# Prompt attention of a hybrid decoder trunk: bias add and row maximum in one vector operation per bank, from a bias tile that POOL makes per head

## What is computed

```python
dist = (q_pos[:, None] - k_pos[None, :]).astype(jnp.float32)
slopes = alibi_slopes(DA_HEADS)
bias = jnp.where(dist >= 0, -slopes[:, None, None] * dist, -jnp.inf)
s1 = jnp.einsum('bqhd,bkhd->bhqk', q1, k1).astype(jnp.float32) * scale + bias
s2 = jnp.einsum('bqhd,bkhd->bhqk', q2, k2).astype(jnp.float32) * scale + bias
attn = jax.nn.softmax(s1, axis=-1) - lam * jax.nn.softmax(s2, axis=-1)
return jnp.einsum('bhqk,bkhv->bqhv', attn, v.astype(jnp.float32))
```

## Time and profile before

| | |
|---|---|
| median of three runs | 2865.07 us (2863.9 to 2873.49) |
| the profiled execution | 2858.58 us |
| its span on the core | 2856.8 us |
| PE busy | 2757.1 us, 97% of the span |
| DVE busy | 1390.2 us, 49% |
| ACT busy | 1026.7 us, 36% |
| POOL busy | 226.1 us, 8% |

### The profile page before, as it was taken

The page is one execution under the profiler, slowest core; times in us unless marked ns, Lnnn a source line. Parts: engine busy times, 40 slices in busy tenths (PEclk is TensorE's granted clock), DMA queues, the critical chain, the costliest instruction groups (busy, mean ns, idle before and its releaser), DMA issues.

```text
span 2856.8 us, 56783 instructions
## 1 busy us (share of the span) xinstructions
PE 2757.1 (97%) x23882; PEld 2602.8 (91%) x23882; DVE 1390.2 (49%) x1624; ACT 1026.7 (36%) x1155; POOL 226.1 (8%) x140
## 2 busy tenths in 40 slices
PE   7999999999899999999999999999998999999996
PEld 7999999976499999999999999989655999999996
DVE  5333346744666543333653333547356665333345
ACT  5343223312464343332343332333125633343222
POOL 0111001321000011100001100012300000111000
PEclk9999999997999999999999999999889999999998
DMA  4222232256622222222322222323656222222221
GB/s 150 93 88 80 91 124 91 75 173 191 204 96 89 89 89 94 92 81 85 104 89 97 94 72 92 131 76 115 183 174 192 89 82 96 88 88 79 91 96 59
DMA packets 119393, 304.61 MB, mean 107 GB/s; under 512 B 14930, under 2 KB 24914, under 8 KB 118738
## 3 DMA queue, kind: packets, MB, share of 16 engines
q1 hardware_dynamic: 119250, 302.57, 32.8%
HBM read 291.08 MB, written 11.44 MB: 106 GB/s over the span
## 4 chain that ended last, share of the span: by engine, by line
PE 84%; DVE 7%; DVEq 4%; ACT 3%; issue 1%; POOL 0%; DMA 0%; SPq 0%; ACTq 0%; POOLq 0%
PE ps L598 63%; PE ps L646 9%; PE ps L810 2%; DVE wlo L1550 2%; ACT whi L1169 1%; DVEq L1665 1%; PE ps L893 1%; DVEq L2021 1%; PE ps L865 1%; PE ps L959 1%; DVE mx L1879 1%; PE ps L697 1%; PE ps L878 1%; ACT L1169 1%; DVEq L1878 1%
## 5 line engine op out<-in xcount | busy, mean ns | idle before, releaser
L598 PE MATMUL ps<-Hh,whi 128*128 128x260 f32 x3456 | 694.8, 282 | 15.6 <-DVE Hl L1616 13.9
L598 PE MATMUL ps<-Hl,whi 128*128 128x260 f32 x3456 | 693.2, 282 | 0.0
L598 PE MATMUL ps<-Hh,wlo 128*128 128x260 f32 x3456 | 692.1, 282 | 0.0
L1169 ACT ACTIVATE whi<-raw 128x2048 fp32r<-128x2048 f32 (+2 forms) x225 | 395.8, 1759 | 723.2 <-PE ps L598 662.1
L1550 DVE TENSOR_TENSOR wlo<-raw,whi 128x2048 fp32r<-128x2048 f32 (+2 forms) x213 | 444.5, 2087 | 368.5 <-ACT whi L1169 368.4
L598 PEld LDWEIGHTS ps<-Hh,whi 128*128 128x128 f32 x3456 | 530.3, 188 | 16.8 <-issue 13.8
L598 PEld LDWEIGHTS ps<-Hl,whi 128*128 128x128 f32 x3456 | 532.5, 189 | 0.0
L598 PEld LDWEIGHTS ps<-Hh,wlo 128*128 128x128 f32 x3456 | 531.7, 188 | 0.0
L1169 ACT ACT_TABLE_LOAD x169 | 216.8, 1283 | 310.3 <-PE ps L598 231.5
L1550 DVE TENSOR_TENSOR ta<-ps,R 128x520 f32<-128x520 f32 x88 | 61.6, 700 | 475.9 <-PE ps L598 474.8
L598 PE MATMUL ps<-Gh,whi 128*128 128x260 f32 x1408 | 284.0, 283 | 0.0
(11 more groups left out here) (271 smaller groups left out, 3019.7 us busy)
## 6 DMA issues: line engine op xcount, KB each, us to landing
raw<-in_ffn_up SPq DMA_DIRECT2D x176, 512.0 KB, 4.2
raw<-in_ffn_down SPq DMA_DIRECT2D x128, 352.0 KB, 3.3
kb<-in_cache_k SPq DMA_DIRECT2D x128, 256.0 KB, 3.1
kb<-in_cache_v SPq DMA_DIRECT2D x128, 256.0 KB, 3.0
raw<-in_w_in SPq DMA_DIRECT2D x56, 512.0 KB, 4.4
raw<-in_w_gate SPq DMA_DIRECT2D x32, 512.0 KB, 4.8
raw<-in_w_ab SPq DMA_DIRECT2D x16, 512.0 KB, 4.4
raw<-in_w_o SPq DMA_DIRECT2D x16, 512.0 KB, 4.4
```

Of the source, the lines that this page charges most:

```text
L598: last = nc.tensor.matmul(ps[:, bank + 2 * m + c, 0:HT], w, x[:, k0 + k, c * HT:(c + 1) * HT], start=starts and k == 0 and n == 0, stop=st ...
L1169: return nc.scalar.activation(out, in_, func, **kw)
```

## The change

POOL makes one tile per head and layer, `bias` = distances x slope (128 x 512), in two buffers used in turn. The first lies where `Ke` was, which is dead once `kc1` is counted, the second where `NTl` was and `Osb` will be. POOL makes heads 0 and 1 after `kc1`, head 2 after `max03` and head 3 after `max13`, that is, when the last reader of the same buffer is done. On DVE, the two `scalar_tensor_tensor` and the `reduce_max` of an item give way to two `tensor_tensor_reduce`, each of which adds bias and scores, writes `sc`, and gives the maximum over its n columns as an accumulator output; one of the two drains goes. Each head's first item waits for its bias tile. Nothing else of the loop's order is changed.

```diff
--- before.py
+++ after.py
@@ -258,6 +258,7 @@
         Zx, Eb = (at(n, [P, SEQ], F32, tb_at + 2048 * m) for m, n in enumerate(("Zx", "Eb")))
         Es = at("Es", [P, PAST], F32, tmp_at)
         Osb = at("Osb", [P, SEQ], F32, scr_at + 13312)
+        bias = [at(f"bias{n}", [P, SEQ], F32, o) for n, o in enumerate((h_at + 2 * T * 4, scr_at + 13312))]
         qz = at("qz", [P, NSEQ * 129], F32, tb_at)
         vtok = at("vtok", [P, 2, SEQ], F32, tb_at)
         bkm = at("bkm", [16, 4, P], F32, pt_at)
@@ -380,6 +381,7 @@
         a_pe = track("a_pe", "vt0" + "".join(stage(i, "at", "vt", "score", "out") for i in range(NI + 2)) + " out3")
         a_dve = track("a_dve", " ".join((f"attn{item(i - 1)} " if i else "") + (f"max{item(i)}" if i < NI else "") for i in range(NI + 1)))
         a_act = track("a_act", "vt0" + "".join(stage(i, "at", "vt", "exp", "out") for i in range(NI + 2)) + " out3")
+        a_pool = track("a_pool", " ".join(f"b{h}" for h in range(H)))
         n_act = track("n_act", " ".join(f"rt{k - 1} sq{k} yh{k - 1}" if k else "sq0" for k in range(8)) + " rt7 yh7")
         n_pe = track("n_pe", " ".join(f"sum{k}" for k in range(8)))
         n_dve = track("n_dve", " ".join(f"y{k} yl{k}" for k in range(8)))
@@ -1539,6 +1541,14 @@
                 pool.wait_ge(d_pe.sem, d_pe.at("w51", L))
                 nc.gpsimd.memset(Pz[:, :, :], 0.0).then_inc(q_pool.on("pz", L), 1)
 
+                for h in range(H):
+                    if h > 1:
+                        pool.wait_ge(a_dve.sem, a_dve.at(f"max{h - 2}3", L))
+                    elif h == 0:
+                        pool.wait_ge(d_dve.sem, d_dve.at("kc1", L))
+                    nc.gpsimd.tensor_scalar(bias[h % 2][:, :], CM[:, M_DIST:M_DIST + SEQ], CC[:, C_SLOPE + h:C_SLOPE + h + 1], None, ALU.mult
+                                            ).then_inc(a_pool.on(f"b{h}", L), 1)
+
                 ffn(L, B_UP2, 1)
 
 
@@ -1871,12 +1881,11 @@
                         dve.wait_ge(a_pe.sem, a_pe.at(f"at{h}{q - 2}", L))
                     elif h:
                         dve.wait_ge(a_pe.sem, a_pe.at(f"at{h - 1}{q + 2}", L))
+                    if q == 0:
+                        dve.wait_ge(a_pool.sem, a_pool.at(f"b{h}", L))
                     for m in range(2):
-                        V.scalar_tensor_tensor(out=sc[:, q % 2, m, 0:n], in0=CM[:, M_DIST + SEQ - n:M_DIST + SEQ],
-                                               scalar=CC[:, C_SLOPE + h:C_SLOPE + h + 1],
-                                               in1=ps[:, 4 + m, 0:n], op0=ALU.mult, op1=ALU.add)
-                    dve.drain()
-                    V.reduce_max(mx[:, q % 2, :], sc[:, q % 2, :, 0:n], AXX)
+                        V.tensor_tensor_reduce(out=sc[:, q % 2, m, 0:n], in0=bias[h % 2][:, SEQ - n:SEQ], in1=ps[:, 4 + m, 0:n],
+                                               scale=1.0, scalar=NEG, op0=ALU.add, op1=ALU.max, accum_out=mx[:, q % 2, m:m + 1])
                     dve.drain()
                     V.tensor_scalar(nm[:, q % 2, :], mx[:, q % 2, :], -SCALE, None, ALU.mult).then_inc(a_dve.on(f"max{h}{q}", L), 1)
 
```

## The result

| | before | after |
|---|---|---|
| median of seven runs | 2865.95 us (2860.16 to 2876.82) | 2847.91 us (2842.5 to 2856.08) |
| ratio after / before | | 0.9929, 95% interval 0.9908 to 0.9951 |
| the profiled execution | 2858.58 us | 2846.88 us |

The change is faster by 0.7%, 20 us by the ratio; 13.1 us (0.46%) had been forecast. The same two kernels were compared once more at the end of the study, on another chip: 2850.28 us (ten runs) against 2862.28 (fourteen), ratio 0.9958, 0.9944 to 0.9972, that is 12 us. The two intervals overlap between 0.9944 and 0.9951. So the gain is certain, and its size is 12 to 20 us depending on which comparison one takes. The traces show where executions of one kernel differ, and they say more about the forecast's steps than the total does.

What follows compares the result with a forecast made beforehand. The kernel is bound by PE, the attention loop by a chain through PE, DVE and ACT. Per layer 1.05 + 3.52 + 1.97 = 6.5 us, 13.1 for two: 2865.07 - 13.1 = 2852 us, range 2847 to 2864.

Steps and rivals of the forecast that it cites:

- rival 1: On DVE, TTR needs two cycles per element because of its accumulator; 2864 us, or 2870 with a costly read; chance 0.12.
- Rival 2: In the loop, PE, ACT or `S` becomes late at the 512 item too; 6.5 us lost, 2858.5 us; chance 0.10.
- Rival 3: POOL's four tiles per layer each block DVE for 1.27 us, 10 us in all; 2862 us; chance 0.04.
- I take it as long as L1875: On DVE, each TTR takes as long as the L1875 it replaces: 0.74 us with 512 keys, 0.61 with 384.
- two reads are 0.18: On DVE, each item's two accumulator reads put off what follows by 0.09 us each, as on ACT.
- if the read is hidden: Upper bound of DVE's saving per item: reduce + 0.08, that is 0.50, 1.03 or 1.30 us; 16.2 in all.
- The gain should arrive undiminished: Everything behind the attention loop hangs on its end in the same order, so all 13.1 us reach the total.
- SP's loads … come earlier as these do: SP's loads wait for PE's steps and move earlier with them; no DMA is added or moved.
- Head 3's 1.97 us: Gain per layer from head 3's items on the path: 0.85 us with 384 keys plus 1.12 with 512.
- One with a single input should take no longer: A POOL bias tile takes at most the 1.27 us of a two-input operation; DVE's first item waits 0.1 us.
- the 0.2 that the prediction had named as a sign against it: DVE idle time put down to POOL's L1549 above 0.2 us would show the forecast wrong.
- rival 4: Shorter gaps keep PE's clock up in both layers' loops; time falls by more than 20 us further; chance 0.02.

Runs made afterwards that it cites:

- experiment 7: Kernel of experiment 5 with PE's state matmuls ahead of the transposes in all odd items; one execution, 2847.19 us.
- experiment 2: Changed kernel with the fused operation in the 512-key items alone, separate add and reduce in the others; 2852.12 us, ratio 0.9964 to the kernel before.
- experiment 3: Changed kernel with SP loading the last four groups of value pages from fixed numbers, without reading the page table; one execution, 2840.25 us.
- experiment 6: Kernel before the change, with page numbers read into SP's registers ahead of the buffer wait; 2860.82 us, ratio 0.9995.
- experiment 8: Kernel of experiment 7 with POOL's first tile made in two pieces, 128 columns first; 2847.74 us, ratio 0.9945 to the kernel before.
- experiment 9: Changed kernel with ACT issuing one group of pages and page numbers read ahead of SP's wait; 2845.52 us, ratio 0.9939 to the kernel before.
- experiment 5: Changed kernel with a group's four page numbers read into SP's registers ahead of the buffer wait; 2847.34 us, ratio 0.9944 to the kernel before.
- experiment 10: Kernel of experiment 9 plus POOL's first tile in two pieces and state matmuls ahead of transposes in items 3, 7, 11, 15; 2841.14 us, repeat 2839.92.

## Why the forecast was nearly right in the sum and wrong in three terms

**Right.** The loop is a chain, and the gain comes from the items of it, not from DVE's share: PE's busy time stayed, DVE's fell. The 384 item of heads 1 and 2 is held at 0.31 us by PE's L989, which is 0.32 as forecast, and that it is L989 is shown by experiment 7, where moving that matmul freed 0.37. The fused operation runs at full rate. With that rival 1 falls. Rival 2, PE, ACT or `S` late at the 512 item too, falls for heads 1 and 2 by experiment 2, where 1.40 + 0.24 should arrive and 1.65 did. In head 3 its outcome came by a wait that it didn't name, that for the last pages. Rival 3 falls: the later tiles are never waited for. With one source in PSUM the accumulator's form takes 1.03 ns a column. The Trainium skill's rule of half rate with two SBUF sources that aren't bf16 ("Vector Engine (DVE) Microarchitecture Reference", points that are easy to get wrong) doesn't hold in this trace for the plain form: L1891 has both sources in SBUF in fp32 and takes 0.75 us, full rate. TTR says nothing against it, since one source is in PSUM; no run here had the accumulator with both in SBUF.

**The price of TTR with its read: mis-sized.** The step was "I take it as long as L1875" and "two reads are 0.18". TTR is 0.06 shorter than L1875, twice per item, and the reads cost 0 instead of 0.18. Together 0.30 us per item on the path: 0.60, 1.12 and 1.40 us instead of 0.32, 0.85 and 1.12. The head distance, forecast at -1.76, was -2.39; over two distances in each layer that is 2.5 us of gain that the forecast lacked. The row for it stood in the trace of before, in the earlier trace rows: `S<-Sd,ps`, a plain sum of an SBUF and a PSUM stream of 512 columns on the same engine, takes 0.68 us against L1875's 0.74. It was read as the scan's business, and L1875 taken because it was the operation being replaced. For the read, ACT's row was taken as nearest "since it is the same kind of instruction"; on DVE it starts together with the next operation. The bound "if the read is hidden" was the right end; added up over the items on the path it gives 16.0 us for two layers, not the 16.2 of the prediction.

**"The gain should arrive undiminished" and "SP's loads … come earlier as these do": wrong.** Head 3's 1.97 us, with true prices 2.5, was lost in full. SP's loads do come earlier, as PE's release does, but the release is not moved by head 3's later items: it lies ahead of them, and the eight issues and the transfer behind it last 12.3 us in both kernels. The step looked for what waits for DVE, ACT and PE, and never followed the queue that fills `kb`. Experiments 3 and 6 show both sides: with shorter issues the 2.5 us arrive, and in the kernel before the same relief is worth nothing.

**POOL's tile: mis-sized.** "One with a single input should take no longer" than 1.27 us; it took 1.56. The wait was 0.54 instead of 0.1, above the 0.2 that the prediction had named as a sign against it, but only at a layer's first item. Experiment 8 removed it.

**The clock, given little.** From head 0 to head 1 the change saved 1.8 to 2.0 us. In layer 0 half of it is DVE's: from the first score operation of the 384 item to the end of its `sc` it is 4.58 us (696.98 to 701.56) instead of 5.58 (694.94 to 700.52). The rest comes behind that, where the chain is PE alone up to head 1's 384 item: 19.75 us instead of 20.71 for the same matmuls. Some of the transposes among them, at 1.2 GHz before, ran at the higher clock (chain rows, first before, then after):

```profile
700.57 0.90 PE ps L692 x3
...
711.90 1.05 PE ps L692 x4
```

```profile
701.61 0.55 PE ps L694 x3
...
712.55 0.59 PE ps L694 x4
```

Granted clock in windows of this stretch (columns of the earlier trace rows), first before, then after:

```profile
695.00:700.00 5.00, 3.74 (x14) 1.54 (x13) 4.61 (x12) 1.57 (x5) 0.00 (x0) 0.50 0.35 104
700.00:705.00 5.00, 4.43 (x25) 2.67 (x25) 3.69 (x7) 1.59 (x5) 0.00 (x0) 0.50 0.01 3
705.00:710.00 5.00, 5.00 (x27) 2.88 (x27) 2.63 (x8) 1.64 (x6) 0.00 (x0) 0.50 0.00 0
```

```profile
695.00:700.00 5.00, 4.65 (x24) 2.42 (x22) 3.76 (x13) 1.57 (x5) 0.00 (x0) 0.62 0.99 298
700.00:705.00 5.00, 3.39 (x21) 1.91 (x22) 3.13 (x11) 1.89 (x5) 1.56 (x1) 0.72 0.04 11
705.00:710.00 5.00, 5.00 (x28) 3.04 (x27) 2.14 (x10) 1.28 (x4) 0.00 (x0) 0.50 0.00 0
```

Before, PE runs at 0.50 (1.2 GHz) for about 24 us, from 689.5 to 713. After, the clock is up in between for some 4 us around 700, and about 17 us are left at 1.2 GHz. The rise in between, with PE idle for half of it, isn't what counts: in layer 0 of the repeat it is missing (0.50 from 692.3 to 712.8), and the stretch took 24.37 us as well. There too the low clock ended earlier in the work, 14.9 us behind the start of the 384 item, against 18.1 before. Nothing like the 20 us of rival 4 came of it, but the clock is a large source of spread: with the same DVE work the stretch took 22.9 us in both layers of experiment 3 and in layer 1 of experiment 9, 24.4 in the change, and 27.4 and 20.5 in the two layers of experiment 8. A difference of a few us between two profiled executions can come from here alone.

It doesn't explain why the two comparisons differ by 8 us. In all four traced loops of the change this stretch took 24.3 to 24.4 us, and the repeat's two loops are 2.7 us longer, 2.4 of it in the tails. By the medians, 3.7 us lie between the two results of the kernel before and 2.4 between those of the change. The intervals overlap, so chance is enough for it; no run here shows another cause.

**The sum.** By the means of the four loops the forecast was too small by 0.4 us a layer up to head 0's 384 item, by 1.0 from there to head 1's (the clock and, in layer 1, a pause of before among it) and by 1.6 to head 3's (0.35 of it a pause of before, the rest twice the 0.63 of the head distance), and too large by 2.4 behind that: 7.2 us a layer where 6.5 was forecast. 2852 us compares with 2847.91 as the median, 1 us inside the range; by the two ratios, put on the 2865.07 of before, with 2844.7, 2 us below the range, and 2853.0. The sum came out near because errors cancelled, which was luck, and only the cuts by stretch show it. The first stretch was 1.2 us longer in layer 1 of before than in its layer 0; the granted clock was 0.50 for some 9 us of it there and for 6 in layer 0, which may be the cause and wasn't tested.

## What to carry to other kernels

When a chain is shortened, follow also the buffers that its steps free: which queue refills them, how long its issues last one after another, and whether that path was level with the chain before. For the price of a new operation, look for rows of the same engine with the same number of operands and the same memories before taking the operation it replaces, and bound each unknown from such rows on the same engine. Where the total can come out right by cancelling errors, check the forecast stretch by stretch; and where several small limits are level, remove them together and compare on one chip, for each alone may be too small to tell from the spread.

## What was not expected of the hardware

- On DVE the accumulator read (83 ns) began at the same time as the next operation (721.84 for both), while on ACT the next exponential began 0.09 us behind the read the earlier trace rows.
- `scalar_tensor_tensor` with a per-partition scalar took 0.06 us more than `tensor_tensor` of two streams of the same kind, with 512 columns (742 against 681 ns) as with 384 (612 against 551).
- POOL took 1.56 us for 128x512 with one tensor and a per-partition scalar, and 1.27 for two tensors.
- SP needed 1.1 us for a load whose page number it first reads into a register, and eight in a row stood on the critical path for 8.8 us. Issued closer together, the last load landed later behind its issue: 4.9 us instead of 3.4 (experiment 5).
- Wherever POOL was still at work on head 1's tile, a DVE operation on 128x32 (`Co`) took 0.51 instead of 0.24 us and ended 0.04 us behind POOL: in both layers of experiment 8, in layer 1 of experiment 10 and in both of its repeat. `Cm`, of the same form and just ahead of it, kept its 0.24 us beside the same POOL operation. In the trace of experiment 8:

```profile
690.08 0.24 DVE L1866 TENSOR_SCALAR Cm<-CM,cf 128x32 f32<-128x32 f32 x1
...
690.40 0.51 DVE L1868 TENSOR_SCALAR Co<-Cm,eo 128x32 f32<-128x32 f32 x1
```

In experiment 9 and in layer 0 of experiment 10, where POOL was done before it, it took 0.24.
